# A mixer and mixture-of-experts layer on one core: the last expert pair's outputs added on TensorE, the other rows loaded earlier, and the scratch rows zeroed in the first half

## What is computed

```python
h = layer_norm(ALPHA * h + mix, ln1_g, ln1_b)
# ffn: for both chosen experts e of a token
y = (silu(x @ w1[e]) * (x @ w3[e])) @ w2[e]      # 2048 -> 512 -> 2048
ffn = e_w[0] * y[first choice] + e_w[1] * y[second choice]
h = layer_norm(ALPHA * h + ffn, ln2_g, ln2_b)
```

## Time and profile before

| | us |
|---|---|
| median of 3 runs | 2145.46 (2145.35 to 2146.33) |
| the profiled execution | 2144.49 |
| its span, first to last instruction | 2142.70 |
| TensorE matmuls busy | 2056.4 (96%) |
| VectorE busy | 1593.0 (74%) |
| ScalarE busy | 1272.4 (59%) |
| PoolE busy | 106.0 (5%) |

### The profile page before, as it was taken

The page is one execution under the profiler, slowest core; times in us unless marked ns, Lnnn a source line. Parts: engine busy times, 40 slices in busy tenths (PEclk is TensorE's granted clock), DMA queues, the critical chain, the costliest instruction groups (busy, mean ns, idle before and its releaser), DMA issues.

```text
span 2142.7 us, 29970 instructions
## 1 busy us (share of the span) xinstructions
PE 2056.4 (96%) x11454; PEld 1742.3 (81%) x11454; DVE 1593.0 (74%) x1412; ACT 1272.4 (59%) x1060; POOL 106.0 (5%) x77
## 2 busy tenths in 40 slices
PE   8999999999999999999999999999999999999992
PEld 8998888899999998887887778777777778777861
DVE  7646654453636375445669999999999999999997
ACT  5435663333332323333347888888888888888872
POOL 1000000000000000001000000000000000000001
PEclk9999999999999999999999999999999999999996
DMA  6545335655454544557758999999999999999993
GB/s 214 156 139 159 118 119 185 209 178 176 143 172 156 158 156 156 187 188 242 237 217 316 413 421 421 421 422 418 422 420 418 415 423 420 417 417 419 418 414 149
DMA packets 164608, 602.50 MB, mean 281 GB/s; under 512 B 20321, under 2 KB 28657, under 8 KB 113425
## 3 DMA queue, kind: packets, MB, share of 16 engines
q1 hardware_dynamic: 160816, 593.81, 72.9%
q0 software_dynamic: 3712, 7.59, 1.2%
HBM read 595.05 MB, written 18.89 MB: 287 GB/s over the span
## 4 chain that ended last, share of the span: by engine, by line
PE 66%; DVE 16%; issue 8%; DMA 7%; ACT 3%; DVEq 0%; POOLq 0%; POOL 0%; SPq 0%; ACTq 0%
PE ps L1851 19%; PE ps L1832 15%; DVE wl L702 10%; DMA raw<-in_w_dram 7%; PE ps L1024 6%; PE ps L1025 5%; PE ps L2202 4%; PE ps L1021 4%; ACT wh L562 2%; PE ps L1046 2%; PE ps L1957 2%; PE ps L1937 2%; PE ps L994 1%; PE ps L1924 1%; DVE yall L858 1%
## 5 line engine op out<-in xcount | busy, mean ns | idle before, releaser
L702 DVE TENSOR_TENSOR wl<-raw,wh 128x2048 fp32r<-128x2048 f32 x351 | 789.8, 2289 | 37.6 <-ACT wh L562 36.3
L562 ACT ACTIVATE wh<-raw 128x2048 fp32r<-128x2048 f32 x351 | 668.9, 1915 | 137.6 <-DMA raw<-in_w_dram 77.1
L1422 DVE TENSOR_TENSOR wl<-raw,wh 128x2048 fp32r<-128x2048 f32 (+1 forms) x168 | 379.9, 2264 | 284.4 <-ACT wh L1224 284.3
L1224 ACT ACTIVATE wh<-raw 128x2048 fp32r<-128x2048 f32 (+1 forms) x168 | 318.1, 1896 | 444.7 <-DMA raw<-in_w_in_dram 271.8
L1024 PE MATMUL ps<-wh,xg 128*128 128x512 f32 x896 | 372.1, 415 | 22.1 <-DVE wl L702 21.7
L1025 PE MATMUL ps<-wl,xg 128*128 128x512 f32 x896 | 350.8, 392 | 0.0
L1832 PE MATMUL ps<-hth,wh 128*128 128x272 f32 (+1 forms) x896 | 259.7, 290 | 3.2 <-DVE wl L1422 1.8
L1832 PE MATMUL ps<-htl,wh 128*128 128x272 f32 (+1 forms) x896 | 255.8, 285 | 0.0
L1832 PE MATMUL ps<-hth,wl 128*128 128x272 f32 (+1 forms) x896 | 255.6, 285 | 0.0
L1024 PEld LDWEIGHTS ps<-wh,xg 128*128 128x128 f32 x896 | 168.6, 188 | 74.1 <-DVE wl L702 27.8
L1024 PE MATMUL ps<-wh,hx 128*128 128x512 f32 x508 | 202.1, 398 | 3.5 <-issue 2.4
(11 more groups left out here) (351 smaller groups left out, 3065.5 us busy)
## 6 DMA issues: line engine op xcount, KB each, us to landing
raw<-in_w_dram SPq DMA_DIRECT2D x384, 1024.0 KB, 10.2
raw<-in_w_in_dram SPq DMA_DIRECT2D x103, 1024.0 KB, 5.1
raw<-in_w_pa_dram SPq DMA_DIRECT2D x16, 1024.0 KB, 5.0
raw<-in_w_pb_dram SPq DMA_DIRECT2D x16, 1024.0 KB, 5.0
raw<-in_w_out_dram SPq DMA_DIRECT2D x16, 1024.0 KB, 5.2
raw<-in_w_ukv_dram SPq DMA_DIRECT2D x8, 1024.0 KB, 5.3
yrow<-yscr SPq DMA_DIRECT2D x4, 1024.0 KB, 7.8
raw<-in_w_uq_dram SPq DMA_DIRECT2D x8, 384.0 KB, 3.5
```

The source lines that it names most:

```text
L562: nc.scalar.activation(wh2[:, x % HELD, :], raw2[:, slot2(x), :], ACT.Copy).then_inc(s_wh2, 1)
L702: nc.vector.tensor_tensor(wl2[:, slot2(x), :], raw2[:, slot2(x), :], wh2[:, x % HELD, :].bitcast(F32), ALU.subtract).then_inc(s_wl2, 1)
L1224: nc.scalar.activation(wh[:, n % RING1, 0:c], raw1[:, n % RING1, 0:c], ACT.Copy).then_inc(s_wh, 1)
L1422: nc.vector.tensor_tensor(wl[:, n % RING1, 0:c], raw1[:, n % RING1, 0:c], wh[:, n % RING1, 0:c].bitcast(F32), ALU.subtract).then_inc(s_wl, 1)
```

## The change

**Last pair.** Each expert's 64 output rows now lie on their own partitions of one tile (`own_rows`): `yall` is 128 rows. The last pair's 128 rows are not scattered. In the last pair TensorE transposes that pair's one-hot slots, ScalarE copies them out (`selt`, scaled by 1/ALPHA) with a rounded identity (`identr`); after the last unit TensorE adds up in PSUM, for each tile of tokens, the stream's two halves (`stream_back`, identity times `xh1` and `xl1`, read with 32 x 16 elements out of order) and the last pair's rows (`last_pair_back`, in fp32), four banks a tile. Tile 0's stream stands inside the round; the rest stands behind the branch at the round's end. VectorE adds the two choices' rows from `yrow` (`choices`), then ALPHA times each bank (`collect`), in pieces of 512 columns.

**Rows of the other pairs.** PoolE's marker waits for all scatters but the last pair's and for the units up to the last four; the rows lie where those units' tiles were. `ln2b` moves too.

**Scratch.** Rows of the last pair's tokens must be zero in `yscr`. VectorE zeroes a tile at the start, and SyncE writes it to all 512 rows, four DMAs, between the last query load and the first gate load. VectorE waits for them before `router_sums`, PoolE before the first scatter.

**Routing and the first pair.** Fewer warm-up matmuls, with a wait for each VectorE step; two VectorE operations for the largest count move behind `stream_rest`; ten of the first gathers move behind the first unit; ScalarE rounds the fifth tile before the copies, and the sigmoid of the first expert behind a rounding; VectorE makes the first hidden product a step earlier, and a gather matrix two steps later.

```diff
+        yall = place("yall", [P, D_MODEL], 165888)
+        yrow = place("yrow", [P, TT, 2, D_MODEL], 32768)
+        acc = yrow[:, :, 0, :]
+        zeros = place("zeros", [P, P], 203904)
...
-            pairs(1, PAIRS + 1)
+            pool.wait_ge(s_zs, 16 * (SCRATCH_ROWS // P))
+            pairs(1, PAIRS)
...
-                pool.wait_ge(s_scat[par], 16 * PAIRS * (more + 1))
+                pool.wait_ge(s_scat[par], 16 * PAIRS * (more + 1) - 16)
+            pool.wait_ge(s_used2, 24 * PAIRS * (more + 1) - 4)
...
-                    if k == 14 and early:
-                        sigmoid(2 * turn)
-                    hi(turn, x + HELD)
+                    if x + HELD != HELD or not early:
+                        hi(turn, x + HELD)
+                    if k == 14 and early:
+                        sigmoid(2 * turn)
+                    if k == 10 and last:
+                        act.wait_ge(s_st, rounds)
+                        nc.scalar.activation(identr[:, :], ident[:, :], ACT.Copy)
+                        nc.scalar.activation(selt[:, :], ps[:, 7, 0:SEQ], ACT.Copy, scale=1.0 / ALPHA).then_inc(s_stc, 1)
...
+            routed.extend(range(begun + 1, own.count))
...
-            own.after(nc.vector.scalar_tensor_tensor(r2[:, :, :], pr, 1.0, asg[:, :, :], ALU.add, ALU.mult))
-            nc.vector.tensor_reduce(rs[:, 18:19], ...).then_inc(s_mxr, 1)
             for t in range(TT):
                 stream_rest(t)
+            own.after(nc.vector.scalar_tensor_tensor(r2[:, :, :], rk_[:, :, 0:E], 1.0, asg[:, :, :], ALU.add, ALU.mult))
+            nc.vector.tensor_reduce(rs[:, 18:19], ...).then_inc(s_mxr, 1)
...
-                    if k == 14 and early:
+                    if k == 13 and early:
                         hidden(2 * turn, 0, turn)
...
+            def choices(t):
+                for r in range(2):
+                    dve.wait_ge(s_y[2 * t + r], 16)
+                nc.vector.tensor_tensor(acc[:, t, :], acc[:, t, :], yrow[:, t, 1, :], ALU.add).then_inc(s_yy, 1)
+            def collect(t, c):
+                dve.wait_ge(s_cmb, 4 * t + c + 1)
+                h = slice(512 * c, 512 * (c + 1))
+                fin.after(nc.vector.scalar_tensor_tensor(acc[:, t, h], ps[:, FINAL_BANK[t][c], :], ALPHA, acc[:, t, h],
+                                                         ALU.mult, ALU.add))
...
-            keep_warm(24)
+            keep_warm(12)
             for step_ in routed:
                 pe.wait_ge(s_dve, step_)
-                keep_warm(3)
+                keep_warm(1)
...
                     if early and k == 0:
+                        for q in range(2, 7):
+                            first_gather(q, 1, (1,))
+                    if early and k == 1:
                         pe.wait_ge(s_xg, 1)
                         for h in range(2):
                             first_gather(7, h, (0, 1))
...
+            def stream_back(t):
+                for c in range(4):
+                    for h, src in enumerate((xh1, xl1)):
+                        nc.tensor.matmul(ps[:, FINAL_BANK[t][c], :], identr[:, :],
+                                         src[:, t, :, 32 * c:32 * (c + 1)].rearrange("q k p -> q p k"),
+                                         start=h == 0, stop=False, skip_group_check=True)
+            def last_pair_back(t):
+                for c in range(4):
+                    nc.tensor.matmul(ps[:, FINAL_BANK[t][c], :], selt[:, P * t:P * (t + 1)], yall[:, 512 * c:512 * (c + 1)],
+                                     start=False, stop=True, skip_group_check=True).then_inc(s_cmb, 1)
...
-                for par in range(2):
-                    pe.wait_ge(s_ye[par], last + 1)
+                pe.wait_ge(s_ye[0], last + 1)
+                stream_back(0)
+                pe.wait_ge(s_ye[1], last + 1)
...
             more = pe.value_load(nxi[0:1, 0:1], min_val=0, max_val=ROUNDS - 1)
             with pe.If(more > 0):
                 with pe.Fori(0, more) as r:
-                    one_round(PAIRS * (r + 1))
+                    one_round(PAIRS * (r + 1), r + 2)
+            last_pair_back(0)
+            stream_back(1)
+            last_pair_back(1)
...
+            sp.wait_ge(s_zt, 1)
+            for r in range(SCRATCH_ROWS // P):
+                sp.dma_start(yscr[P * r:P * (r + 1), :].rearrange("p (b c) -> p b c", c=P),
+                             zeros[:, :].unsqueeze(1).broadcast_to([P, KD, P])).then_inc(s_zs, 16)
             with sp.Fori(1, 4 + 1) as i:
                 job(N_GA, i - 1, w_in, C_GA + 512 * i - 512)
```

More of the change, by code:

```diff
@@ L440, in moe_trunk @@
         LAST_BANK = (0, 1, 6, 7)
+        FINAL_BANK = ((2, 3, 4, 5), LAST_BANK)
         routed = []
@@ L595, in last_outputs, with pair @@
                     h = slice(D_MODEL // 2 * c, D_MODEL // 2 * (c + 1))
[L596 to L599 removed]
+                    r = own_rows(1)
+                    nc.scalar.activation(yall[r, h].rearrange("p (b c) -> p b c", b=2), ps[r, b:b + 2, :],
+                                         ACT.Copy, scale=wsc[r, 1:2]).then_inc((s_yh, s_yc)[c], 1)
+            def pair(turn, par, first=False, early=None, last=False, rounds=None):
                 for x in body(first):
@@ L627, in pair, with one_round @@
                             gathered(turn + 1, 1 - par, q)
-            def one_round(turn, early=None):
+            def one_round(turn, rounds, early=None):
                 if not early:
@@ L640, in one_round @@
                 pair(turn + PAIRS - 2, 0)
-                pair(turn + PAIRS - 1, 1, last=True)
+                pair(turn + PAIRS - 1, 1, last=True, rounds=rounds)
                 last_outputs(turn + PAIRS - 1)
@@ L728, in vector_experts @@
             routed.append(own.count)
+            begun = own.count
             for t in range(TT):
@@ L865, in pair @@
                         select(turn, p)
-                    if k == 0 and first:
+                    if k == 2 and first:
                         gather_matrix(turn + 1, 2 * p + 2)
@@ L1051, in mix, with pair @@
                 m.then_inc(s_hm, 1)
-            def pair(turn, par, first=False, early=False, last=False):
+            def pair(turn, par, first=False, early=False, last=False, rounds=None):
                 for x in body(first):
@@ L1097, in pair @@
                     if k == (14 if early else 12):
-                        mix(turn, j, 0, (s_hp, j) if last else (s_xg, 8 * (turn + 1) + 4))
+                        mix(turn, j, 0, *([(s_hp, j), (s_stc, rounds)] if last else [(s_xg, 8 * (turn + 1) + 4)]))
                     if k == 20 and last:
                         mix(turn, j + 1, 1, (s_hp, j + 1))
+                    if k == 8 and last:
+                        pe.wait_ge(s_pd, turn + 1)
+                        pe.wait_ge(s_hp, j)
+                        for t in range(TT):
+                            m = nc.tensor.transpose(ps[:, 7, P * t:P * (t + 1)],
+                                                    pd[:, t, :, :].rearrange("p a s -> p (a s)")[:, SLOTS:3 * SLOTS],
+                                                    ident[:, :])
+                        m.then_inc(s_st, 1)
                     for q in range(8):
@@ L1425, in _ @@
             nc.vector.memset(half[:, :], -0.5).then_inc(s_half, 1)
+            nc.vector.memset(zeros[:, :], 0.0).then_inc(s_zt, 1)
             for c, s in enumerate((s_oa, s_ob, s_g, s_m)):
```

96 lines of the change are left out of this document (51 added, 45 removed).

## The result

| | median, us | lowest to highest | runs |
|---|---|---|---|
| before | 2145.43 | 2144.39 to 2147.78 | 8 |
| after | 2151.80 | 2150.98 to 2154.38 | 8 |

The kernel after is slower: ratio 1.0030, 95% interval 1.0021 to 1.0038, which is 4.5 to 8.2 us. Forecast were +5.1 us and 2150.6. The profiled execution took 2150.98 with a span of 2149.2, 6.5 more than before, and by it the difference is followed here. One stage after the other, an operation is compared with the same one before; what its delay grows by is what the stage costs.

The account below looks back on a forecast made before the run. TensorE was taken to set the pace in the first half, the weights' DMA in the expert stage. Routing -1.2, stall +5.8, clock +2.6, end -2.1 gave +5.1 us: 2150.6 against the median, range 2137.8 to 2157.6.

Parts of the forecast that it names:

- zeros, last query packet to last zero: Before the first gate load: the four zero writes, 4.19 MB, take 13 us, ends 10.0 and 15.1.
- stall of TensorE: At the first gate unit: the load lands late behind the zeros, TensorE goes on at 181.5, not 175.70: +5.8 us.
- clock behind the stall: After TensorE's wait for the first gate load: restarting from rest at a lower clock adds 2.6 us, 0 if under 2.8.
- hidden product sooner: First expert pair: with one VectorE split fewer in front, TensorE's wait for the hidden product shrinks by 1.0 us.
- first part: Routing and first units: earlier start and refill of the weight loads gain 1.2 us, ends 0 and -2.
- last output to TensorE's start: End: after wait, register load and branch, TensorE's remaining work begins at 2110.2, 4.9 us after the last output.
- four fp32 matmuls and clock: End, TensorE behind the branch: four fp32 matmuls of 512 columns take 3.4 us, and the clock after rest adds 2.6.
- strided stream of the second tile: End, TensorE: eight matmuls reading with 512 B between elements take 3.7 us, twice the weights' time, ends 1.9 and 7.4.
- end: From the last output to VectorE's statistics: done at 2126.4 instead of 2128.53, -2.1 us, ends -6.5 and +1.6.
- rival (b): Gate load: the zeros don't hold it, as writes leave engines free for reads; 2142.2, at best 2137.8 us; chance 0.28.
- the dry spell only moves: First expert pair: the DMA queue's dry 1.3 us near 1165 only shifts, so the gain there is 0, its bound.
- rival (c): End: the second tile's stream is a new bound at 1.8 ns an element; +8.8 us, 2154.3; chance 0.06.

Follow-up runs that it names:

- e2_other_queue: The kernel after, with the same four zero writes at the same moment, but issued by PoolE on its own queue: 2151.16 us, ratio 1.0029 to before.
- e8_all: The kernel after, with zero writes spread behind gate loads, ScalarE's sigmoid ahead of the rounding, TensorE's combination ahead of its branch: 2137.57 us, ratio 0.9953 to before.
- e9_before_zeros: The kernel before, with only the zeroing added, at the place where the change has it: 2155.21 us, ratio 1.0036 to before.

## Why the prediction was right, point by point

| step | forecast, us | measured, us |
|---|---|---|
| zeros, last query packet to last zero | 13 (10.0 to 15.1) | 13.2 |
| stall of TensorE | +5.8 (2.8 to 7.9) | +6.18 |
| clock behind the stall | +2.6 (0 to 2.6) | +1.26 |
| rank matmuls, low parts, first unit sooner | 1.3, 1.6, 1.5 | 1.3, 1.7, 1.6 |
| hidden product sooner | 1.0 | 0.98 |
| first part | -1.2 (-2 to 0) | +0.61 at load 28, +1.29 at the last weights |
| last output to TensorE's start | 4.9 | 4.81 |
| four fp32 matmuls and clock | 3.4 + 2.6 | 5.16 |
| strided stream of the second tile | 3.7 (1.9 to 7.4) | 4.63 |
| end | -2.1 (-6.5 to +1.6) | -2.01 |
| sum | +5.1 | +6.4 (medians), +6.5 (profiled) |

**The zeroing** was right in mechanism and size. The price between the query packets' share and whole rows, 13 us, is what the writes took, and nothing but the slack of 4.4 us hid any of it. The query packets were a weak row for it, since 560 of the 1584 were under 512 B; the zeros' own 347 GB/s bear the reading out. The reason given against rival (b), "one queue", was not the one that decides: e2_other_queue is just as late. **Its clock** was mis-sized. The prediction took 2.6 us from the program's first burst and applied it whole. Its lower end, no loss under a stall of 2.8 us, is not safe either: a rest of 2.69 us was followed by a clock of 0.50 in eight traces (last section). The row to price it by is a stretch at 0.50 multiplied by what TensorE does in it: of the 7 us at the low level its weight matmuls ran in the last 3 only, 0.43 us apart instead of 0.23.

**The first part** is the step that failed, and it fell outside its own bounds. Every time up to the hidden product is within 0.15 us. The step that failed is "What it wins back is the hidden product. One split fewer, 2.2 us, stands in front of it". It counted the split's way out of the front and not its arrival behind, and counted the sigmoid's delay for TensorE alone. In that stretch VectorE is the bound: before, it splits without a gap longer than 0.4 us. Its wait of 1.1 us for the sigmoid is time that nothing gives back; the first output and the split after it come later, and the weights that wait for the freed slots with them. The part behind is the larger: the split that comes later adds 1.6 us between the hidden product and the first output, the wait for the sigmoid 1.1 ahead of it, and 2.2 was all that there was to win. The bound "0 (the dry spell only moves)" was too good as well: the spell broke into shallower pieces, some of them later, and load 28 came 0.61 late. Nor was a time won or lost at that point "kept up to the last weights": e8_all is 0.56 ahead at load 28 and level at the end.

**The end** came out at the forecast with its terms: the branch is the new wait and costs what it cost before, to 0.1 us; the clock took less (1.8 instead of 2.6) and the strided stream more (4.63 instead of 3.7). The second tile's stream reads at 0.53 us per 512 columns where weights take 0.23, 2.3 times, between the bounds of once and of VectorE's 1.8 ns an element (1.04 here). The Trainium skill's penalty for an access that goes on to another 16-byte line ("SBUF — State Buffer", Door 1: The DMA port swizzle) agrees in kind; rival (c), which took VectorE's size for it, is refuted.

So the total is within 1.4 us in part by luck. Two errors of opposite sign stand in it, the clock behind the stall 1.3 too high and the first part 2.5 too low, and so do two times of the clock at places that the change doesn't touch, -0.95 and +0.87.

## What to carry to other kernels

Scratch that is cleared ahead of a load costs that load the whole time of the writes, less its slack, on both queues tried here; put one write into each gap of the loads instead, where the gap is longer than the write. When a step is moved, ask for each engine it touches whether that engine has idle time there: on one that has none, a new wait of 1 us is 1 us of the end, even if another engine gains by the move. Work that a branch leads to in every case belongs ahead of the branch.

## What was not expected of the hardware

The clock after one and the same rest falls in one execution and not in the next. Where the merged stream is turned, TensorE has waited 2.69 us in both kernels; before it goes on at 1.00, after at 0.50, which costs 0.87; of the 13 traces of this case 8 have the fall and 5 have not, with the same rest in each. All eight are of kernels with the four zero writes together in front of the gate load, which nine of the kernels have; of the four without, none has it. Each kernel was traced once, so whether that stall has a part in the fall is not shown. TensorE's timeline and a stretch of the kernel before, then both of the kernel after:

```profile
1003.65 4.13 PE L2168 MATMUL ps<-ident,mrg 128*128 128x128 f32 x32 [2.69 <-DVE mrg L1606]
```
```profile
1004.00:1005.00 1.00, 1.00 (x11) 1.00 (x10) 0.46 (x2) 0.88 (x4) 1.00 (x3) 1.00 1.06 414
```
```profile
1010.01 5.37 PE L2236 MATMUL ps<-ident,mrg 128*128 128x128 f32 x32 [2.69 <-DVE mrg L1673]
```
```profile
1011.00:1012.00 1.00, 1.00 (x7) 1.00 (x6) 0.84 (x2) 0.89 (x3) 1.00 (x2) 0.50 1.03 389
```

The same shows near the end of the expert stage (a wait of 2.67 us at 2061 before, clock 1.00; of 2.70 at 2071 in e9_before_zeros, clock 0.50, 3 us lost), and in the first burst of the program, 40 records in 7.21 us before and 6.16 after, 6.10 to 7.52 in the 13 traces whatever the kernel; that is the 0.95 at the start. Executions of one kernel lie up to 8 us apart (35 of the kernel before on one chip: 2144.10 to 2152.35), and the long ones have a lower mean granted clock: of 15 on another chip, the four at 0.991 have a median of 2144.4, the three at 0.987 of 2150.3. A change of 1 us is therefore read from the stage's own rows, not from two totals.

The branch that leads to nothing costs TensorE 3.80 us after and 3.87 before; no run took it away, only the work behind it.
